# Two transformer blocks in one kernel: column halves, half squares and another root at the boundaries of the second block

## The reference

```python
h = rmsnorm_2(x, g_pre[l, 0]) * (1 + sc1) + sh1
x = x + 0.5 * gt1 * rmsnorm_2(swiglu_2(h, w_gu1[l], w_dn1[l]), g_post[l, 0])

h = rmsnorm_2(x, g_pre[l, 1]) * (1 + sc2) + sh2
y = token_mixer(h, w_in[l], w_a2[l], b_a[l], b_f[l], g_gla[l], w_pa[l], w_pb[l], w_out[l])
x = x + gt2 * rmsnorm_2(y, g_post[l, 1])

h = rmsnorm_2(x, g_pre[l, 2]) * (1 + sc3) + sh3
x = x + 0.5 * gt3 * rmsnorm_2(swiglu_2(h, w_gu2[l], w_dn2[l]), g_post[l, 2])
```

## Time and profile before

| | |
|---|---|
| median of three runs | 1366.82 us (1366.34 to 1368.17) |
| the profiled execution | 1367.43 us |
| its span in the trace | 1365.6 us |
| TensorE matmul busy | 1341.1 us, 98% of the span |
| VectorE busy | 932.5 us, 68% |
| ScalarE busy | 747.1 us, 55% |
| granted TensorE clock | 1.00 (mean of the core) |
| DMA | 270.87 MB, mean 198 GB/s |

### The profile page before, as it was taken

How to read it: one execution, slowest core, us unless ns; L and a number is a source line. 1 busy time by engine, 2 the same in 40 slices (tenths; PEclk the granted TensorE clock), 3 DMA queues, 4 the chain that set the end, 5 groups by cost and what they waited for, 6 DMA issues and landing times.

```text
span 1365.6 us, 17135 instructions
## 1 busy us (share of the span) xinstructions
PE 1341.1 (98%) x6583; PEld 1116.7 (82%) x6583; DVE 932.5 (68%) x1339; ACT 747.1 (55%) x1151; POOL 67.8 (5%) x131
## 2 busy tenths in 40 slices
PE   7999999999999999999999999999999999999998
PEld 5888888878888888888788887789988888688886
DVE  5778757857566878857778875678866456765543
ACT  5545447557774644446744544766457664754442
POOL 3101000000000010000000000100000000000000
PEclk9999999999999999999999999999999999999999
DMA  9898766543375788865588875565543355456662
GB/s 280 291 295 277 250 191 196 170 123 98 99 250 182 227 287 285 279 231 169 170 277 264 290 234 169 168 177 157 168 139 109 108 169 170 155 184 185 185 189 88
DMA packets 167120, 270.87 MB, mean 198 GB/s; under 512 B 14242, under 2 KB 114826, under 8 KB 167040
## 3 DMA queue, kind: packets, MB, share of 16 engines
q1 hardware_dynamic: 154240, 226.66, 53.5%
q0 software_dynamic: 12496, 42.65, 9.4%
q10 hardware_dynamic: 304, 0.48, 0.1%
HBM read 268.66 MB, written 1.05 MB: 198 GB/s over the span
## 4 chain that ended last, share of the span: by engine, by line
PE 93%; ACT 3%; DVE 3%; DMA 1%; issue 1%; SPq 0%; POOL 0%; DVEq 0%; ACTq 0%
PE ps L1880 26%; PE ps L1845 16%; PE ps L1847 16%; PE ps L1846 16%; PE ps L2049 2%; PE ps L1859 1%; PE ps L2060 1%; PE ps L1860 1%; PE ps L1861 1%; PE ps L2357 1%; PE ps L1950 1%; PE ps L1952 1%; PE ps L1951 1%; PE ps L1968 1%; DMA raw<-in_ffn_wgu_dram 1%; PE ps L2132 1%
## 5 line engine op out<-in xcount | busy, mean ns | idle before, releaser
L1099 DVE TENSOR_TENSOR w_lo<-raw,w_hi 128x1024 fp32r<-128x1024 f32 (+2 forms) x431 | 515.2, 1215 | 246.2 <-ACT w_hi L619 244.6
L619 ACT ACTIVATE w_hi<-raw 128x1024 fp32r<-128x1024 f32 (+2 forms) x431 | 447.5, 1054 | 343.6 <-DMA raw<-in_ffn_wgu_dram 96.7
L1845 PE MATMUL ps<-w_hi,a_hi 128*128 128x512 f32 (+1 forms) x976 | 392.0, 402 | 2.2 <-DVE w_lo L1099 1.9
L1847 PE MATMUL ps<-w_hi,a_lo 128*128 128x512 f32 (+1 forms) x976 | 380.6, 390 | 0.0
L1846 PE MATMUL ps<-w_lo,a_hi 128*128 128x512 f32 (+1 forms) x976 | 379.4, 389 | 0.0
L1847 PEld LDWEIGHTS ps<-w_hi,a_lo 128*128 128x128 f32 x976 | 183.8, 188 | 39.1
L1845 PEld LDWEIGHTS ps<-w_hi,a_hi 128*128 128x128 f32 x976 | 184.2, 189 | 38.5 <-DVE w_lo L1099 3.6
L1846 PEld LDWEIGHTS ps<-w_lo,a_hi 128*128 128x128 f32 x976 | 184.3, 189 | 34.7
L1880 PE MATMUL ps<-w_hi,hid_hi 128*128 128x512 f32 x316 | 98.1, 392 | 0.0
L1880 PE MATMUL ps<-w_lo,hid_hi 128*128 128x512 f32 x316 | 97.4, 389 | 0.0
L1880 PE MATMUL ps<-w_hi,hid_lo 128*128 128x512 f32 x316 | 97.4, 389 | 0.0
(11 more groups left out here) (406 smaller groups left out, 1587.8 us busy)
## 6 DMA issues: line engine op xcount, KB each, us to landing
raw<-in_ffn_wgu_dram SPq DMA_DIRECT2D x176, 256.0 KB, 4.4
raw<-in_w_in_dram SPq DMA_DIRECT2D x88, 512.0 KB, 3.7
raw<-in_w_gu_dram SPq DMA_DIRECT2D x176, 256.0 KB, 3.5
ada<-in_w_ada_dram POOLq DMA_DIRECT2D x72, 512.0 KB, 5.6
raw<-in_ffn_wdown_dram SPq DMA_DIRECT2D x44, 512.0 KB, 4.3
raw<-in_w_dn_dram SPq DMA_DIRECT2D x44, 512.0 KB, 4.3
raw<-in_w_in_dram SPq DMA_DIRECT2D x36, 256.0 KB, 3.1
raw<-in_w_out_dram SPq DMA_DIRECT2D x16, 512.0 KB, 4.3
```

The costliest lines, as they stand in the source:

```text
L619: act.activation(w_hi[:, u % RING, 0:nk * n], raw[:, u % RING, 0:nk * n], ACT.Copy).then_inc(hi_ready, 1)
L1099: dve.tensor_tensor(w_lo[:, u % RING, 0:nk * n], raw[:, u % RING, 0:nk * n], w_hi[:, u % RING, 0:nk * n].bitcast(F32), ALU.subtract).then_ ...
L1845: pe.matmul(dst(t)[:, 0:n], a[0], slot(u, w_hi, kk, n), start=kc == 0, stop=False)
L1847: i = pe.matmul(dst(t)[:, 0:n], a[1], slot(u, w_hi, kk, n), start=False, stop=kc == KC - 1)
```

## The change

Five things change; the inverse root changes everywhere it is used, the rest at the two boundaries of the second block:

1. `last_halves` replaces `last_rows`: the last four row blocks are done for tile 0 left half, tile 0 right half, tile 1 left half, tile 1 right half, with a `first_tile` signal after each of the first three. The units are marked used only in the last of the four passes.
2. The squares of both norms are taken by halves. From the first half's row sum VectorE makes a bias (`half_bias`: sum times 0.25 / D plus 0.25 EPS), which ScalarE then adds to the second half's sum inside the square root.
3. The inverse root is refined on the root a (of a quarter of the mean): r = 1 / a, a + v r, and 1 / that, which is again a Newton step. On one column that is four VectorE instructions, on more than one five.
4. The order on VectorE changes: only one gated half of tile 1 before the scaling of tile 0; the other half after it; the root of tile 1 behind the first low part of tile 0. On ScalarE the first two chunks of tile 0 are shifted before the root of tile 1.
5. The fillers become 4 and 4 instead of 13 and 15.

```diff
 def last_halves(u0, n, hi, lo):            (new, TensorE)
+    for t in range(T):
+        for half in range(2):
+            for k in range(n - SKEW, n):
+                if t == 0 and half == 0:
+                    pe.wait_ge(lo_ready, u0 + k + 1)
+                i = row_quarter(u0 + k, k, t, half, n - 1, hi, lo)
+                if t == 1 and half == 1:
+                    i.then_inc(used, 1)
+            if t == 0 or half == 0:
+                i.then_inc(sem("first_tile"), 1)

-            busy(13, 7)
+            busy(4, 7)
             turn_tile("mix2", h, 0)
...
-            last_rows(u_wo2, KC, a_hi, a_lo)
-            busy(15, 7)
+            last_halves(u_wo2, KC, a_hi, a_lo)
+            busy(4, 7)
             turn_tile("f3", h, 0)

 inverse_root (VectorE)
+                if bias is None:
+                    then(dve.tensor_scalar(v, src, 0.25 * scale, 0.25 * EPS, ALU.mult, ALU.add))
+                else:
+                    then(dve.scalar_tensor_tensor(v, src, 0.25 * scale, bias, ALU.mult, ALU.add))
                 dve.wait_ge(sem("sqrt_ready"), ROOTS.index(key) + 1)
                 then(dve.reciprocal(dst, a))
-                then(dve.tensor_tensor(a, dst, dst, ALU.mult))
-                then(dve.scalar_tensor_tensor(a, a, -0.5, v, ALU.mult, ALU.mult))
-                i = dve.scalar_tensor_tensor(dst, a, 1.5, dst, ALU.add, ALU.mult)
+                if src.shape[-1] == 1:
+                    then(dve.scalar_tensor_tensor(a, v, dst, a, ALU.mult, ALU.add))
+                else:
+                    then(dve.tensor_tensor(v, v, dst, ALU.mult))
+                    then(dve.tensor_tensor(a, a, v, ALU.add))
+                then(dve.reciprocal(dst, a))

 post_and_norm (ScalarE)
-                act.wait_ge(sem("first_tile"), FIRST_TILE[prev])
-                post_tile(prev, 0)
-                norm_tile(key, 0)
-                norm_root(key, 0)
-                act.wait_ge(used, end)
-                act.wait_ge(sem("post_made"), 4 * POST[prev])
-                post_tile(prev, 1)
-                tile_hi(key, 0)
-                norm_tile(key, 1)
-                norm_root(key, 1)
+                done, biases = FIRST_TILE[prev], 4 * (POST[prev] - 1)
+                act.wait_ge(sem("first_tile"), done - 1)
+                post_squares(0, 0)
+                act.wait_ge(sem("first_tile"), done)
+                post_squares(0, 1)
+                act.wait_ge(sem("pss_ready"), pss_at(prev, 0))
+                biased_root(f"{prev}_post0", pss, 0, 0, biases + 1)
+                norm_squares(key, 0)
+                act.wait_ge(sem("ss_ready"), ss_at(key, 0))
+                biased_root(f"{key}_0", ss, 0, 2, biases + 2)
+                act.wait_ge(sem("post_made"), 4 * (POST[prev] - 1) + 3)
+                post_squares(1, 0)
+                act.wait_ge(used, end)
+                post_squares(1, 1)
+                tile_hi(key, 0, 0, 2)
+                act.wait_ge(sem("pss_ready"), pss_at(prev, 1))
+                biased_root(f"{prev}_post1", pss, 1, 1, biases + 3)
+                tile_hi(key, 0, 2)
+                norm_squares(key, 1)
+                act.wait_ge(sem("ss_ready"), ss_at(key, 1))
+                biased_root(f"{key}_1", ss, 1, 3, biases + 4)
                 tile_hi(key, 1)

 post_and_norm (VectorE)
-                dve.wait_ge(sem("pss_ready"), 2 * POST[prev] + 1)
+                biases = 4 * (POST[prev] - 1)
+                dve.wait_ge(sem("pss_ready"), pss_at(prev, 0, 0))
+                half_bias(0, biases + 1)
                 gated(prev, 0, 0)
+                dve.wait_ge(sem("pss_ready"), pss_at(prev, 0))
                 gated(prev, 0, 1)
                 post_root(prev, 0)
                 post_sum(prev, 0, 0)
                 post_sum(prev, 0, 1)
-                dve.wait_ge(used, end)
+                dve.wait_ge(sem("ss_ready"), ss_at(key, 0, 0))
+                half_bias(2, biases + 2)
+                dve.wait_ge(sem("first_tile"), FIRST_TILE[prev] + 1)
                 gated(prev, 1, 0)
-                gated(prev, 1, 1)
                 tile_root(key, 0)
                 dve.wait_ge(sem("x_ready"), 4 * NORM[key] - 2)
                 normalise(key, 0)
+                dve.wait_ge(sem("pss_ready"), pss_at(prev, 1, 0))
+                half_bias(1, biases + 3)
+                dve.wait_ge(sem("pss_ready"), pss_at(prev, 1))
+                gated(prev, 1, 1)
+                chunk_lo(key, 0, 0)
                 post_root(prev, 1)
-                chunk_lo(key, 0, 0)
+                chunk_lo(key, 0, 1)
                 post_sum(prev, 1, 0)
-                chunk_lo(key, 0, 1)
                 tile_lo(key, 0, 2, 4)
                 post_sum(prev, 1, 1)
-                tile_lo(key, 0, 4)
+                tile_lo(key, 0, 4, 6)
+                dve.wait_ge(sem("ss_ready"), ss_at(key, 1, 0))
+                half_bias(3, biases + 4)
+                tile_lo(key, 0, 6)
                 tile_root(key, 1)
```

More of the change, by code:

```diff
@@ L183, in two_blocks @@
         half_ss = keep("half_ss", [P, 2])
+        first_half = keep("first_half", [P, 4])
+        root_bias = keep("root_bias", [P, 4])
         kd, KD0, _ = place("kd", [P, GH * S])
@@ L422, in two_blocks, with pss_at, ss_at @@
         SKEW = 4
-        FIRST_TILE = {k: i + 1 for i, k in enumerate(["f0", "merge", "wo", "f1", "emb", "f2", "merge2", "mix2", "f3"])}
+        FIRST_TILE = {"f0": 1, "merge": 2, "wo": 3, "f1": 4, "emb": 5, "f2": 7, "merge2": 9, "mix2": 11, "f3": 13}
+        def pss_at(key, t, half=1):
+            return {"f2": 2, "mix2": 6}[key] + 2 * t + half + 1 if key != "f3" else 10 + t + 1
+        def ss_at(key, t, half=1):
+            q = NORM[key]
+            return 2 * q + t + 1 if q < 5 else 10 + 4 * (q - 5) + 2 * t + half + 1
         def group(key):
@@ L632, in square_root, with post_squares, norm_squares, biased_root @@
             def square_root(key, dst, src, scale):
-                act.activation(dst, src, ACT.Sqrt, scale=scale, bias=epsb[:, 0:1]).then_inc(sem("sqrt_ready"), 1)
+                act.activation(dst, src, ACT.Sqrt, scale=0.25 * scale, bias=epsb[:, 0:1]).then_inc(sem("sqrt_ready"), 1)
             def post_tile(key, t):
                 act.activation(junk[:, :], wide(t), ACT.Square, accum_out=pss[:, t:t + 1]).then_inc(sem("pss_ready"), 1)
-                act.wait_ge(sem("pss_ready"), 2 * POST[key] + t + 1)
+                act.wait_ge(sem("pss_ready"), pss_at(key, t))
                 square_root(f"{key}_post{t}", rt[:, 1, t:t + 1], pss[:, t:t + 1], 1.0 / D)
+            def post_squares(t, half):
+                of = first_half[:, t:t + 1] if half == 0 else pss[:, t:t + 1]
+                act.activation(junk[:, 512 * half:512 * half + 512], acc(t, half), ACT.Square, accum_out=of).then_inc(sem("pss_ready"), 1)
+            def norm_squares(key, t):
+                for half in range(2):
+                    c = slice(512 * half, 512 * (half + 1))
+                    of = first_half[:, 2 + t:3 + t] if half == 0 else ss[:, t:t + 1]
+                    act.wait_ge(sem("x_ready"), 4 * (NORM[key] - 1) + 2 * t + half + 1)
+                    act.activation(h[:, t, c], x[:, t, c], ACT.Square, accum_out=of).then_inc(sem("ss_ready"), 1)
+            def biased_root(key, src, t, bias, count):
+                act.wait_ge(sem("root_bias"), count)
+                act.activation(rt[:, 1, t:t + 1], src[:, t:t + 1], ACT.Sqrt, scale=0.25 / D, bias=root_bias[:, bias:bias + 1])\
+                   .then_inc(sem("sqrt_ready"), 1)
             def norm_tile(key, t):
@@ L658, in first_norm, with tile_hi @@
                     act.activation(h[:, t, :], x[:, t, :], ACT.Square, accum_out=ss[:, t:t + 1]).then_inc(sem("ss_ready"), 1)
-            def tile_hi(key, t):
+            def tile_hi(key, t, c0=0, c1=KC):
                 n = group(key)
-                for c in range(0, KC, n):
+                for c in range(c0, c1, n):
                     act.wait_ge(sem("turned"), 8 * TURN[key] + 4 * t + (c + n) // 2)
@@ L1087, in _ @@
             act.activation(junk[:, 512:], acc(1, 1), ACT.Square, accum_out=pss[:, 1:2]).then_inc(sem("pss_ready"), 1)
-            act.wait_ge(sem("pss_ready"), 2 * POST["f3"] + 2)
+            act.wait_ge(sem("pss_ready"), pss_at("f3", 1))
             act.wait_ge(sem("emb_ready"), T + 1)
-            act.activation(rt[:, 1, 1:2], pss[:, 1:2], ACT.Sqrt, scale=1.0 / D, bias=half_ss[:, 1:2]).then_inc(sem("sqrt_ready"), 1)
+            act.activation(rt[:, 1, 1:2], pss[:, 1:2], ACT.Sqrt, scale=0.25 / D, bias=half_ss[:, 1:2]).then_inc(sem("sqrt_ready"), 1)
         @block.vector
@@ L1153, in tile_root @@
                 c = slice(t, t + 1)
[L1154 to L1155 removed]
+                dve.wait_ge(sem("ss_ready"), ss_at(key, t))
+                inverse_root(f"{key}_{t}", rstd[:, c], ss[:, c], 1.0 / D, [rt[:, 0, c], rt[:, 1, c]],
+                             root_bias[:, 2 + t:3 + t] if NORM[key] >= 5 else None)
             def tile_lo(key, t, c0=0, c1=KC):
```

(10 more changed lines are left out.)

39 lines of the change are left out of this document (18 added, 21 removed).

## The result

The changed kernel is slower. Its median is 1371.74 us (1369.64 to 1376.43, 20 runs) against 1367.40 us (1366.04 to 1373.09, 20 runs) for the kernel before on the same chips: ratio 1.0029, interval 1.0022 to 1.0036. The forecast was 1364.1, in a range to 1366.2. The profiled execution took 1371.29 us, span 1369.5.

What follows compares the result with a forecast made beforehand. TensorE, busy for 98% of the span, was taken as the bound, with gains only where it does no useful work; 1.8 + 0.6 + 0.19 + 0.1 = 2.7 us off 1366.82 gave 1364.1, range 1363.0 to 1366.2.

Steps and rivals of the forecast that it cites:

- TensorE's term: Tail of the down projections: halves keep the same 48 matmuls and the same loads, priced at 0.
- The sum: Whole kernel: 1.8 + 0.6 + 0.19 + 0.1 = 2.7 us gained.
- The bounds: Gain of 0.7 to 2.3 us at the first boundary, 0.2 to 1.2 at the second, together with the tail 1.0 to 3.8.
- The change does nothing: Rival, chance 0.06: a wait put down as hidden, such as a late weight or bias, takes the whole gain; 1366.8 us.
- The first boundary: f2 to mix2: tile 1's transposes come 1.8 us earlier, 1.55 if a pause before the scaling stays.
- The second boundary: mix2 to f3: DVE starts at 1162.29 as before, tile 1's scaling comes at 1174.85 instead of 1175.45, 0.6 us gained.
- The halves bring tile 0 nothing at the second boundary: mix2 to f3: ACT's square starts only after its conversions, when both halves of tile 0 are there; no gain.
- The root at the end: End of the kernel: the final tile's root loses one DVE step, 0.19 us.
- The fillers as a cover: Both boundaries: fillers cover the chain, so cutting them is worth only what the chain becomes shorter.
- Late release of four units: Tail: four weight loads start up to 2.0 us later, but hidden, costing nothing.
- The clock: Rival, chance 0.04: TensorE falls to 1.2 GHz at the boundaries; 1373.7 us at both, 1368.9 at one alone.
- The queue on DVE: Rival, chance 0.24: DVE's queue leaves tile 1 only 0.62 us at each boundary, + 0.3: gain 1.5 us, 1365.3.

Runs made afterwards that it cites:

- after_old_places: Changed kernel with its two new buffers in unused space of existing ones, so every other buffer stands where it stood before; 1364.96 us, ratio to before 0.9982.
- after_old_places_12: Changed kernel with the buffers in the old places and 12 fillers instead of 4 before f3; 1364.09 us, ratio 0.9977.
- after_root_back: Changed kernel with the old places and tile 1's post root back ahead of the first low part on VectorE, ScalarE's root likewise moved; 1365.74 us, ratio 0.9993.

## Why the prediction was wrong, point by point

**The failed step is TensorE's term, put at nothing.** The sum priced TensorE's part as "the same 48 matmuls and the same loads: 0", and gave no price to the two new buffers at all. The matmuls are the same in number, but in the four down projections each takes 6.4 ns longer, 6.8 us in all. The declaration of the buffers was the dearest line of the change: 6.7 us as a part alone, against 2.5 that all the rest brings. The bounds were bounds of the instructions at the boundaries, and so the range missed. "The change does nothing" looked for mishaps in the same places.

**The first boundary (1.8 forecast): right.** With the buffers in place tile 1's transposes went from 10.16 to 8.44 after the tail, 1.7. The middle stretch says the same: 314.46 to 312.72. The steps hold too: from tile 0's first low part to the last square of tile 1's new x 3.48 us (3.49 forecast), from there to the scaling 1.80 (1.75 forecast). In the changed kernel it was 2.2: DVE starts 5.0 before the end of the tail there, 4.6 in `after_old_places` and 4.1 before; that the slower tail gives it the time is likely and not shown.

**The second boundary (0.6 forecast): wrong by its starting point.** Not a step of the chain failed: from DVE's first gated half to tile 1's transposes were 13.70 us before (13.5 to 13.6 in the six other profiles of the old order), and are 13.1 in the changed kernel and 13.0 in `after_old_places_12`. But I let DVE start at 1162.29 "as before". That moment hangs on the landing of a load: 3.49 us before the end of the tail in the one profile that I had, and 2.66 to 3.38 in the six others of the kernel before with other places or fillers. Mine was the earliest of seven. With 2.8, as in the changed kernel and in `after_old_places`, the half microsecond is gone.

**The halves bring tile 0 nothing at the second boundary: right**, and the cause named (conversions in the way) was worth more than the forecast of the whole boundary; I took it as given instead of pricing it.

**The root at the end: 0.19 forecast, 0.12 measured.** Four steps aren't four times 0.19, as one of them takes 0.06 longer.

**The fillers as a cover: right** for the chain, from both sides; that they also keep the clock up had no price in the sum. **Late release of four units: right**, no wait for w_lo grew (1.11 us before, 1.14 and 1.10 in the changed kernel and `after_old_places`, behind the second boundary).

**The clock (0.04): it fell**, in three profiles at the place named, and by the runs' mean clocks in 40 of 64. So its chance was far too low, and its price too high: I took a whole tile's matmuls at half rate, 4.8 us; the fall cost 0.15 to 1.6 in the profiles and about 1 between the runs, as most of the slow matmuls lay under VectorE's chain. The row that I followed (0.83 us of idling) was too short a gap to speak for one of 2. The Trainium skill ("TensorE: Matmul & The Clock Gate", Part 1) says that the moment at which the clock rises differs from run to run, since the hardware watches the engine in a rhythm of its own. No run here shows that rhythm, but one kernel falling in some runs and not in others fits it. The fall isn't why the kernel is slower: with the buffers mended and the clock still falling it is faster than before.

**The queue on DVE (0.24)** did not eat the gain: it would have left 0.62 at the first boundary, and 1.7 came. What the moved root costs there is 0.19 us per boundary by `after_root_back`, in the trace alone.

**The sum: 2.7 forecast**, 2.5 (1.2 to 3.7) measured with the buffers in the old places. That agreement is partly luck: 0.6 of the sum wasn't there, and the clock took something in 8 of the 11 runs. The traces place 1.7 us in the middle stretch and nothing in the last; where the rest of the 2.5 lies, if it isn't noise, they don't show, since the first stretch varies by more than that.

## What to carry to other kernels

A new buffer is part of a change, however small: compare the addresses behind it, and read the mean durations of instructions that weren't touched before reading those that were. Put small late additions where nothing stands behind them, or into the padding of others, and for float32 products like these keep the operands that TensorE reads together at a distance that is a multiple of 256 bytes. A part that leaves TensorE idle is judged over several runs and their granted clocks, since one profile may or may not show the fall. And a moment that hangs on a transfer's landing needs several profiles before half a microsecond is built on it.

## What the runs showed of the hardware

A matmul of 128x512 in this float32 form comes every 227 ns with the stationary tile at its old distance from the streamed weight or 256 bytes off it (as I take it from the allocation, both then start equally far from a multiple of 256), and every 233 ns when it is moved by 64 or 128. The Trainium skill, "SBUF — State Buffer", section "Operand start alignment", asks only for a start at a multiple of the element size, and says that it speaks of legality and not of speed; both places satisfy it, and the kernel's times differ by 0.5%. It happens with ScalarE and VectorE idle too. Other distances weren't tried, and why it happens isn't shown; neither is which of the two reads is slowed, nor whether the transfers that run beside have a part in it. The other surprise was the granted clock: after 2.0 to 2.4 us without work it fell to half, for 3.4 to 6.8 us in three profiles, and did not in two; by the mean clocks it fell in 40 of 64 runs, in some runs of a kernel and not in others.
